# A last RMSNorm and transpose moved into the last group of an MLP down-projection, block by block

## The reference, cut to what matters

```
def _rmsnorm(x, g):
    xf = x.astype(jnp.float32)
    r = xf * lax.rsqrt(jnp.mean(xf * xf, axis=-1, keepdims=True) + EPS)
    return (r * g.astype(jnp.float32)).astype(x.dtype)
...
    hf = _rmsnorm(x, norm_ffn_g)
    a = jax.nn.relu(jnp.einsum('btd,df->btf', hf, w_up))
    x = x + jnp.einsum('btf,fd->btd', a * a, w_down)
...
    y_prompt = _rmsnorm(xp, norm_final_g)
    y_sample = _rmsnorm(xs, norm_final_g)
```

## Time and profile before

| | |
|---|---|
| median of 3 runs | 1686.42 us |
| lowest run | 1681.87 us |
| profiled execution, its own time | 1685.24 us |
| span of its slowest core (core 5) | 1683.6 us |
| spans of its 8 cores | 1667.5 to 1683.6 us |
| mean granted TensorE clock of the cores | 0.802 to 0.809 |

### The profile page before, as it was taken

One profiled execution on the slowest core, in us unless ns is written; L12 is line 12 of the kernel. 1 busy time (PEld: TensorE's weight loads), 2 busy tenths in 40 slices (PEclk: granted clock), 3 DMA queues, 4 the chain that ended last, 5 costly groups with the idle time before them and its releaser, 6 DMA issues.

```text
span 1683.6 us, 21508 instructions; the slowest of 8 cores (1667.5 to 1683.6 us)
## 1 busy us (share of the span) xinstructions
PE 1131.3 (67%) x6487; PEld 596.0 (35%) x6487; DVE 647.6 (38%) x1390; ACT 661.2 (39%) x1210; POOL 53.6 (3%) x92
## 2 busy tenths in 40 slices
PE   5420336776666755165968676289999999999844
PEld 4210214554445543121313232034444444444323
DVE  2211342444344443224344534331452353254544
ACT  2321334445434452126263543466325424523133
POOL 0000001101111011000000000000000000000000
PEclk8665557987889887676959787579999999999966
DMA  8584210000000000624150412600212221210022
GB/s 249 180 241 147 70 35 1 1 1 1 1 0 1 1 1 4 203 100 150 51 200 20 181 65 86 199 1 26 76 29 97 76 77 49 75 51 1 1 100 102
DMA packets 45590, 124.26 MB, mean 74 GB/s; under 512 B 3511, under 2 KB 12375, under 8 KB 45446
## 3 DMA queue, kind: packets, MB, share of 16 engines
q1 hardware_dynamic: 45478, 122.88, 22.1%
HBM read 110.03 MB, written 13.30 MB: 73 GB/s over the span
## 4 chain that ended last, share of the span: by engine, by line
PE 53%; DVE 16%; ACT 10%; DMA 9%; issue 8%; POOL 2%; SPq 1%; DVEq 1%; ACTq 0%; POOLq 0%
PE ps L236 50%; DVE junk L886 3%; PE ps L239 2%; DVE hT L257 2%; DMA stg<-w_in 2%; ACT sq L242 2%; ACT L242 2%; DVE yT L257 2%; DMA xrow<-xp 1%; ACT rst L242 1%; POOL tB L248 1%; POOL tA L248 1%; DVE hfT L257 1%; DMA stg<-w_qm 1%; DVE t L257 1%
## 5 line engine op out<-in xcount | busy, mean ns | idle before, releaser
L248 DVE TENSOR_TENSOR xT<-ps,xT 128x512 f32<-128x512 f32 (+2 forms) x432 | 230.6, 553 | 285.6 <-PE ps L236 270.2
L236 PE MATMUL ps<-hfT,wu 128*128 128x512 bf16 (+1 forms) x1280 | 237.7, 346 | 12.8 <-DVE wu L263 12.8
L236 PE MATMUL ps<-a,wd 128*128 128x512 bf16 (+1 forms) x1280 | 228.4, 337 | 0.0
L236 PE MATMUL ps<-hT,win 128*128 128x256 bf16 (+3 forms) x936 | 126.6, 290 | 71.8 <-DVE hT L257 48.4
L236 PE MATMUL ps<-sq,ones_bf 128*128 128x512 bf16 (+2 forms) x200 | 72.1, 381 | 141.7 <-ACT sq L242 133.8
L236 PEld LDWEIGHTS ps<-hfT,wu 128*128 128x128 bf16 x1280 | 109.4, 99 | 141.2 <-issue 25.5
L236 PEld LDWEIGHTS ps<-a,wd 128*128 128x128 bf16 x1280 | 106.9, 97 | 121.1
L242 ACT ACTIVATE sq<-xT 128x512 bf16<-128x512 f32 (+2 forms) x192 | 83.9, 482 | 112.7 <-DVE xT L248 57.2
L236 PEld LDWEIGHTS ps<-hT,win 128*128 128x128 bf16 (+1 forms) x936 | 89.8, 106 | 97.2 <-issue 79.1
L242 ACT ACTIVATE rr<-ps 128x512 f32<-128x512 f32 (+1 forms) x160 | 81.7, 511 | 63.5 <-PE ps L236 63.3
L242 ACT ACTIVATE a<-rr 128x512 bf16<-128x512 f32 (+1 forms) x160 | 87.5, 547 | 15.0 <-ACT rr L242 0.4
(11 more groups left out here) (176 smaller groups left out, 1299.5 us busy)
## 6 DMA issues: line engine op xcount, KB each, us to landing
Kt<-ck SPq DMA_DIRECT2D x16, 1024.0 KB, 5.1
Vt<-cv SPq DMA_DIRECT2D x16, 1024.0 KB, 7.2
stg<-w_up SPq DMA_DIRECT2D x16, 1024.0 KB, 6.2
stg<-w_down SPq DMA_DIRECT2D x16, 1024.0 KB, 5.2
stg<-w_in SPq DMA_DIRECT2D x16, 516.0 KB, 7.1
xrow<-xp SPq DMA_DIRECT2D x16, 512.0 KB, 5.8
y_p<-yrow SPq DMA_DIRECT2D x16, 512.0 KB, 2.7
stg<-w_km SPq DMA_DIRECT2D x4, 1024.0 KB, 12.6
```

The source lines that it names most:

```text
L236: S.add('pe', lambda e: e.matmul(out, lhsT=lhsT, rhs=rhs, start=start, stop=stop), reads=reads, writes=[wb])
L248: S.add(eng, lambda e: e.tensor_tensor(out=out, in0=in0, in1=in1, op=op), reads=reads, writes=writes)
```

## The change

The loop over the groups calls `down` for the groups 0 to 6 only. In the last group, for the blocks in the order 4, 0, 1, 2, 3, a new `down_block` does the down-projection of that block alone (all 8 output chunks), and a new `final_block` then does the norm, transposes, copies and the DMA of the block. The barrier and the separate final pass are gone. The norm goes by pieces of 256 tokens in place of 512. Its output lies in the first staging buffer (one `yT` in place of two), the rows lie in the two halves of the second one (two row buffers in place of four). One VectorE memset of a single column ties the old users of that buffer to the two new row buffers.

```
@@
+            def down_block(fg, b):
+                j = fg % 2
+                t0, n = blocks[b]
+                for ct in range(8):
+                    ps, Bp = nps()
+                    for ft in range(4):
+                        MM(ps[:, 0:n], wd[j][:, ft, ct * 128:(ct + 1) * 128], a2[j][:, ft, t0:t0 + n], ft == 0, ft == 3,
+                           [B_wd[j], B_a2[j][b]], Bp)
+                    add_into_x(ps, Bp, ct, t0, n)
+
+            yTv = stg[0][:, :].rearrange("p (c t) -> p c t", c=8)
+            yrow = [stg[1][:, 0:1024], stg[1][:, 1024:2048]]
+            fin_k = [0]
+
+            def final_block(b):
+                t0, n = blocks[b]
+                for h0 in range(0, n, 256):
+                    nh = min(256, n - h0)
+                    rmsnorm(ntmp3, xT[:, :, t0 + h0:t0 + h0 + nh], xbufs(t0 + h0, nh), 4, yTv[:, :, 0:nh], B_stg[0], nh)
+                    tw = min(nh, 128)
+                    for tt in range(max(1, nh // 128)):
+                        i = fin_k[0] % 2
+                        fin_k[0] += 1
+                        for half in range(2):
+                            ps, Bp = nps()
+                            for c4 in range(4):
+                                TR(ps[0:tw, c4 * 128:(c4 + 1) * 128], yTv[:, half * 4 + c4, tt * 128:tt * 128 + tw], ident[:, :],
+                                   [B_stg[0], B_c], Bp)
+                            CP(('act', 'dve')[half], yrow[i][0:tw, half * 512:(half + 1) * 512], ps[0:tw, :], [Bp], [B_yr[i]])
+                        if n == NS:
+                            DMA('sp', y_s, yrow[i][0:tw, :], [B_yr[i]], [], is_output=True)
+                        else:
+                            r0 = t0 + h0 + tt * 128
+                            DMA('sp', y_p[r0:r0 + 128, :], yrow[i][:, :], [B_yr[i]], [], is_output=True)
@@
             for fg in range(NG):
                 if fg + 1 < NG:
                     up(fg + 1)
-                down(fg)
+                if fg < NG - 1:
+                    down(fg)
+                else:
+                    B_yr = [Buf(), Buf()]
+                    S.add('dve', lambda e: e.memset(stg[1][:, 0:1], 0.0), reads=[], writes=[B_stg[1], B_yr[0], B_yr[1]])
+                    for b in (4, 0, 1, 2, 3):
+                        down_block(fg, b)
+                        final_block(b)
                 if fg + 2 < NG:
                     load_group(fg + 2)
-            S.barrier()
-
-        cut(31)
-        with ExitStack() as es4:
...
-            yT2 = [sb(es4, f"yT{i}", [128, 8, 512], F32) for i in range(2)]
-            B_yT2 = [Buf(), Buf()]
-            yrow = [sb(es4, f"yrow{i}", [128, 1024], F32) for i in range(4)]
...
-            for b, (t0, n) in enumerate(blocks):
-                yT, B_yT = yT2[b % 2], B_yT2[b % 2]
-                rmsnorm(ntmp, xT[:, :, t0:t0 + n], xbufs(t0, n), 4, yT[:, :, 0:n], B_yT, n)
...
```

More of the change, by code:

```diff
@@ L1048, in build_nc @@
                     up(fg + 1)
-                down(fg)
+                if fg < NG - 1:
[6 more added lines that the diff above has]
+                        final_block(b)
                 if fg + 2 < NG:
                     load_group(fg + 2)
-            S.barrier()
-        cut(31)
-        with ExitStack() as es4:
-            sq = [sb(es4, f"sq4_{i}", [128, 512], BF16) for i in range(2)]
-            rstd = sb(es4, "rstd4", [128, 512], F32)
-            ntmp = (sq, [Buf(), Buf()], rstd, Buf())
-            yT2 = [sb(es4, f"yT{i}", [128, 8, 512], F32) for i in range(2)]
-            B_yT2 = [Buf(), Buf()]
-            yrow = [sb(es4, f"yrow{i}", [128, 1024], F32) for i in range(4)]
-            B_yrow = [Buf() for _ in range(4)]
-            k = 0
-            for b, (t0, n) in enumerate(blocks):
-                yT, B_yT = yT2[b % 2], B_yT2[b % 2]
-                rmsnorm(ntmp, xT[:, :, t0:t0 + n], xbufs(t0, n), 4, yT[:, :, 0:n], B_yT, n)
[L1067 to L1080, removed]
         S.finish('sp')
```

## The result

The changed kernel takes 1715.69 us (median of 9 runs) against 1680.79 for the kernel before in the same comparisons. The ratio of the two is 1.0201, with a 95% interval of 1.0189 to 1.0213: 34 us slower, on the line of 2%. Each of the two medians includes one execution that took over 5% longer than the others (1814.64 and 1804.95 us), which the ratio leaves out. Predicted were plus 34 and a range of 1709 to 1735.

What follows compares the result with a forecast made beforehand. The final pass was taken as a chain with one engine working at a time. 10.7 + (8.4 + 1.2 + 27.0) + 3 x (7.2 + 1.2 + 27.0) + 3.9 = 157.4 us against 123.4, plus 34.0: 1720.4; range 1709 to 1735.

Steps and rivals of the forecast that it cites:

- The price of a half: Final norm, block in two halves of 256: 13.25 and 13.75 us, together 27.0 against 20.3 for one piece of 512.
- The rival that halves cost only their share of the columns: Final norm: 20.3 us a block despite the halves, 27 less than forecast, 1693 us; chance 0.05.
- The serial order: TensorE's list in the last group: next down matmuls queue behind the transposes, none under vector work; forecast's chance 0.66.
- The down blocks: 32 down matmuls per block in the last group: 8.4 us for block 0, 7.2 for each of the other three.
- The low-clock rival: Clock stays low in every down block: 4 x 9.0 us, adding 6, so 1726 us; chance 0.2.
- the one slow microsecond: Down block starting behind 16 dense transposes meets about one microsecond of low clock: 7.2 us against 6.9 at full clock.
- The restart: From a block's last down matmul to its first square, a drain and an add: 1.2 us, four times.
- The stretch to replace: From the start of the last down group, 1560.2, to the end of the span, 1683.6: 123.4 us.
- Block 4 and the tail end: Small block 4, first in the last group: 10.7 us; from last transpose to end of span: 3.9 us.
- The barrier: Ahead of the old final pass: 0.98 us before the first square and 1.6 us of TensorE's wait go away.
- The overlap rival: TensorE does each block's down matmuls under the chain of the block before: change of zero, 1687 us; chance 0.05.
- The line of 2%: Whole time: 2% from no change lies at 1720.1 us, splitting the forecast into 0.36 below and 0.30 above.

Runs made afterwards that it cites:

- e1: The kernel before, its separate final pass in pieces of 256 tokens in place of 512: 1705.74 us, ratio 1.0165 to before.
- e2: The changed kernel with the final norm in pieces of 512, two yT and four row buffers: 1681.78 us, ratio 1.0025 to the kernel before.
- e3: The changed kernel with the next block's down matmuls issued between each half's sums and transposes: 1677.69 us, ratio 0.9994 to the kernel before.
- e6: The kernel before without its barrier, final-pass buffers placed where hfT and the up weights lay: 1673.51 us, ratio 0.9962 to before.
- e10: Final pass as chunk-by-chunk pipeline in pieces of 512, down-projection fused in, squares issued one chunk ahead: 1620.39 us, ratio 0.9636 to the kernel before.

## Why the prediction was right

**The price of a half.** Predicted 13.25 and 13.75 us, together 27.0. The timeline after has 1576.35 to 1589.74, 13.4, and on to the last transpose at 1603.68, 13.9: 27.3. Four blocks against 20.3 each were to cost 27; e1 measured 28.0. The rival that halves cost only their share of the columns is out by e1 and e2. The rows explain part of it: a scaling took 0.234 us for 16 columns, 0.484 for 256 and 0.751 for 512, so that about 0.22 of each belongs to the instruction and not to its columns. The Trainium skill (VectorE: DVE Perf Modes, The TRN2 errata) says likewise that such operations pay a fixed cost per instruction, and advises 512 elements or more; the trace agrees.

Not all of the 28 us is such a fixed part. On the slowest core of e1 the 64 scalings take 31.0 us where 32 took 24.0 before, which is 7.0. Its 128 transposes take 29.2 us where the same 128 took 23.4, which is 5.8 and comes from the clock: in pieces of 512 the clock rose before a group of 32 was through, in groups of 16 it is 0.50 throughout (the two groups shown under e1, 3.65 us each). The rest lies in squares, sums and roots. The prediction had the slow transposes in its price (3.0 and 3.8 us), but named only the columns as the reason.

**The serial order.** Predicted: no down matmul under the vector work. The timeline after shows it, and e3 shows that the order of issue was the cause, not a lack of room. No engine waits for a DMA of the row buffers in the last 158 us, as predicted, so the smaller buffers are not the cost.

**The down blocks.** Predicted 8.4 us for block 0 and 7.2 for the others. After: block 0 ended 8.3 us after block 4's last transpose (1566.87 to 1575.18), block 1 7.0 after block 0's, block 2 8.1 (1638.99 to 1647.07), block 3 7.0 (1675.23 to 1682.28). Together 30.4 us where the sum had 30.0. The low-clock rival wanted 9.0 in each and 1726 in all. But the one slow microsecond that the forecast put into each burst is not there. The bursts of blocks 1 and 3 ran at clock 1.00 from their start, block 2's began at 0.50 and had 0.88 in the mean, though all three stood behind the same 3.65 us of transposes at 0.50. That the total fits is in part luck.

**The restart.** Predicted 1.2 us. After: 1575.18 to 1576.35 is 1.2, and 1610.67 to 1611.56 is 0.9.

**Where the last group starts.** The prediction took 1560.2 for it. The first add of the group stands at 1560.39, behind four matmuls of 0.216 us, and counted from it the trace has the 40 adds of the group:

```profile
1560.39 0.69 DVE L248 TENSOR_TENSOR xT<-ps,xT 128x512 f32<-128x512 f32 x1 [0.19 <-PE ps L236]
```

So the group began 1.0 us earlier, at 1559.2, and took 28.6 us, not 27.6. The stretch to replace was 124.4 us, and the sum of the prediction, with nothing else changed, gives plus 33.0. The tails measured plus 32.8. (A smaller slip: the last of the ten slices called nine tenths busy has eight.)

**Block 4 and the tail end.** Predicted 10.7 and 3.9. After: the run of 20 matmuls of 16 columns that starts at 1556.45 has the last four of the group before at its head, so the last group starts at 1556.55, and block 4 took 10.3 to 1566.87. The end came 3.8 after the last transpose at 1710.6. From 1556.55 to 1714.4 is 157.9, where the sum gave 157.4. The absolute time forecast, 1719 to 1720, was some 4 us too high mainly because the kernel before took 1680.79 beside the change and not 1686.42.

**The barrier.** The prediction priced it at 0.98 and 1.6 us. e6 measured 3.8 in the median and 6.0 to 6.6 on three cores, with block 0's transposes nearly 6 us earlier on all; what was left out is that it held back the squares of block 0. That did not touch the forecast, which laid the new stretch out by itself. e2 came out 7 us better than I expected of it, for several reasons: the halves were worth 2 us more than I had put (e1), the barrier at least 1 us more (e6), and I had forgotten that with pieces of 512 the clock is up for the second half of the 32 transposes, so that three of the four down bursts, at 7.07 us, meet no slow matmuls. These do not make up all of the 7.

**The overlap rival** was rightly held unlikely for this order of issue. Its price, a change of zero, is also what e3 measured, but by another sum, as said there.

**The line of 2%.** The forecast put half of the chance on either side of it, and the ratio came out at 1.0201. Within its interval the two sides cannot be told apart.

## What to carry to other kernels

Merging two loops overlaps nothing when each engine works through its own list in order: put the next block's independent work ahead of the wait, between the sums and the transposes here, and look in the trace for the engine that idles with ready work queued behind. Cutting a chain of short instructions in two costs each one's fixed part again, and shorter groups of matmuls can miss the high clock: 28 us here, as much as the fusion could have saved had it hidden all 28.6 us of the last group. After building a pipeline, follow one step from an instruction to its next instance: if no engine is full, some pair stands in the wrong order in a list, and moving it was worth 21 and 29 us here.

## What the runs showed of the hardware

The clock can stand between its two levels, and not only in a stretch in which it changes. In the profiled execution of e10, which took 1630.07 us where its other four runs took 1618.5 to 1621.5, two cores had a tail of 105 us and six of 93 to 95. Ten microseconds in which both run down matmuls, squares and adds, on core 0 and on core 2 (columns as in the stretches above):

```profile
1552.00:1562.00 10.00, 10.00 (x40) 4.15 (x39) 5.71 (x9) 3.15 (x5) 0.00 (x0) 0.81 0.00 0
...
1552.00:1562.00 10.00, 9.81 (x45) 4.38 (x45) 8.06 (x13) 6.23 (x12) 0.00 (x0) 1.00 0.01 2
```

Core 0 stayed at 0.81 in every stretch from 1532 to 1602, in which TensorE was busy 93 to 100%; that is neither 1.2 nor 2.4 GHz. On both cores the level began at 1499, in the up and down groups that all kernels here have in common, and lasted 117 us or more. So the new end did not bring it about. Cores 2 and 3 had it too, but only for 20 and 24 us near the start, from 76 us on. None of the other eleven profiled executions shows it. The Trainium skill (TensorE: Matmul & The Clock Gate, Part 1: The HAM clock gate) names such a level, 13/16, and says it takes the whole die; here cores 2 and 3 of the same die stood at 1.00 at these times, each counted from its own start, so the trace agrees on the level and not on its reach. Why these two cores was not tried.
